# A hybrid decoder step on one core: the sample's attention moved from one 64-column block to four 32-column groups of the array

## The reference

```python
s = jnp.einsum("bqhd,bkhd->bhqk", q_blk, k, preferred_element_type=jnp.float32) * scale
s = s + fq_blk[..., :, None] - fk_t[:, :, None, :]
mask = kpos[None, :] <= pos_blk[:, None]
s = jnp.where(mask, s, -jnp.inf)
pr = jax.nn.softmax(s, axis=-1)
return jnp.einsum("bhqk,bkhd->bqhd", pr.astype(v.dtype), v)
```

## Time and profile before

| | |
|---|---|
| Runs, median (lowest to highest) | 2732.44 us (2732.13 to 2733.84) |
| Profiled execution: span | 2731.8 us |
| Profiled execution: own time | not given apart from its span; the span is 0.6 us under the median of the runs |
| TensorE products (PE) | 2691.7 us busy, 99%, 16935 records |
| Weight loads (PEld) | 2633.0 us, 96% |
| VectorE (DVE) | 1402.5 us, 51% |
| ScalarE (ACT) | 842.8 us, 31% |
| The eight pairs | from 1221 to about 1810 us, 73 to 74 us each |

### The profile page before, as it was taken

One profiled execution on the slowest core, in us unless ns is written; L12 is line 12 of the kernel. 1 busy time (PEld: TensorE's weight loads), 2 busy tenths in 40 slices (PEclk: granted clock), 3 DMA queues, 4 the chain that ended last, 5 costly groups with the idle time before them and its releaser, 6 DMA issues.

```text
span 2731.8 us, 39716 instructions
## 1 busy us (share of the span) xinstructions
PE 2691.7 (99%) x16935; PEld 2633.0 (96%) x16935; DVE 1402.5 (51%) x1960; ACT 842.8 (31%) x1291; POOL 128.8 (5%) x98
## 2 busy tenths in 40 slices
PE   8999999999999999999999999999999999999998
PEld 8999999999999999989989999899999999999998
DVE  6877355244244244347776776756443443442444
ACT  6766321021111111324554455543111211211121
POOL 1000100000000000120000010002000000000000
PEclk9999999999999999999999999999999999999999
DMA  3113111111111111233333333411111111111112
GB/s 132 47 39 107 45 47 40 56 47 40 49 46 42 54 47 35 83 118 94 91 99 98 94 102 98 134 36 55 47 42 54 47 37 52 47 44 52 47 38 81
DMA packets 94354, 174.92 MB, mean 64 GB/s; under 512 B 18402, under 2 KB 55490, under 8 KB 94050
## 3 DMA queue, kind: packets, MB, share of 16 engines
q1 hardware_dynamic: 94178, 172.38, 20.2%
HBM read 145.92 MB, written 18.02 MB: 60 GB/s over the span
## 4 chain that ended last, share of the span: by engine, by line
PE 92%; DVE 4%; ACT 1%; issue 1%; SPq 1%; DMA 0%; DVEq 0%; ACTq 0%
PE psum L421 70%; PE psum L1241 8%; PE psum L1355 2%; PE psum L1385 2%; PE psum L1315 2%; PE psum L1288 2%; PE psum L1328 1%; PE psum L1270 1%; DVE PTL L1829 1%; DVE SB L1811 1%; ACT PTH L1026 0%; DVE QHL L1762 0%; DVE X L1959 0%; ACT SB L1001 0%; PE psum L1102 0%
## 5 line engine op out<-in xcount | busy, mean ns | idle before, releaser
L399 ACT ACTIVATE WH<-WR 128x1024 fp32r<-128x1024 f32 (+2 forms) x221 | 216.2, 978 | 1022.2 <-PE psum L421 973.4
L421 PE MATMUL psum<-XH,WH 128*128 128x352 f32 x2376 | 515.2, 325 | 5.3 <-DVE WL L412 5.3
L421 PE MATMUL psum<-XH,WL 128*128 128x352 f32 x2376 | 512.5, 323 | 0.0
L421 PE MATMUL psum<-XL,WH 128*128 128x352 f32 x2376 | 512.1, 324 | 0.0
L421 PEld LDWEIGHTS psum<-XH,WH 128*128 128x128 f32 x2376 | 405.3, 189 | 5.7 <-DVE WL L412 5.4
L421 PEld LDWEIGHTS psum<-XH,WL 128*128 128x128 f32 x2376 | 408.4, 188 | 0.0
L421 PEld LDWEIGHTS psum<-XL,WH 128*128 128x128 f32 x2376 | 404.1, 188 | 0.0
L1677 DVE TENSOR_TENSOR X<-psum,X 128x1056 f32<-128x1056 f32 x63 | 79.2, 1257 | 371.1 <-PE psum L421 371.1
L412 DVE TENSOR_TENSOR WL<-WR,WH 128x1024 fp32r<-128x1024 f32 (+2 forms) x221 | 246.5, 1115 | 13.7 <-ACT WH L399 13.7
L421 PE MATMUL psum<-FYH,WH 128*128 128x352 f32 x1134 | 245.3, 324 | 0.0
L421 PE MATMUL psum<-FYH,WL 128*128 128x352 f32 x1134 | 244.4, 323 | 0.0
(11 more groups left out here) (267 smaller groups left out, 3739.3 us busy)
## 6 DMA issues: line engine op xcount, KB each, us to landing
WR<-in_wfi SPq DMA_DIRECT2D x96, 512.0 KB, 3.5
WR<-in_wfo SPq DMA_DIRECT2D x64, 384.0 KB, 3.1
WR<-in_wa SPq DMA_DIRECT2D x24, 512.0 KB, 3.5
WR<-in_wqkv SPq DMA_DIRECT2D x24, 512.0 KB, 4.2
X<-in_xT SPq DMA_DIRECT2D x16, 528.0 KB, 5.5
CC<-in_ck SPq DMA_DIRECT2D x128, 64.0 KB, 1.8
CC<-in_cv SPq DMA_DIRECT2D x128, 64.0 KB, 1.9
x_scratch<-X SPq DMA_DIRECT2D x8, 528.0 KB, 6.5
```

The lines of the kernel that those rows point to most:

```text
L399: nc.scalar.activation(WH[:, par, 0:n], WR[:, par, 0:n], ACT.Copy).then_inc(w_hi, 1)
L421: mm = nc.tensor.matmul(psum[0:m, 3 * slot + c, 0:CH], w, x[:, k, c * CH:(c + 1) * CH], start=(k == 0 and part == 0), stop=(k == nk - 1 an ...
```

## The change

The rows of unit 0 now lie over all 128 partitions: four groups of 32 rows (`DG`, `DR`), each with two neighbouring sequences (16 rows) and 16 rows that are not used. The product of sequence b goes with 32 columns of weights to the column group b // 2 of the array (`tile_position`), and in the products with the cache the sequences come in the order 0, 2, 4, 6, 1, 3, 5, 7. In `decode_product` the loop over pages is now outside that over sequences. `SEL`, `QD`, `PTN`, the two page transposes, `DM` and what VectorE and ScalarE read of unit 0 have 128 rows or columns instead of 64; `QXd` and the two `PTX` are smaller (320 numbers per partition instead of 576 and 512). `SEL`, `QD` move to another place in SBUF. The number of products stays the same.

```diff
+DG = 4
+DR = P // DG
+DEC_ORDER = [0, 2, 4, 6, 1, 3, 5, 7]
...
-        QXd = at("QXd", [P, DB, DB * 2 * DS + 2 * DS], F32, o_c)
-        QX = QXd[:, :, :].rearrange("p a b -> p (a b)")[:, 0:2 * NS * DB].rearrange("p (b c) -> p b c", b=DB)
-        DM = at("DM", [2 * NS, DK], F32, o_c + 4 * 576)
+        QXd = at("QXd", [P, DG, 2, DR + 2 * DS], F32, o_c)
+        QX = QXd[:, :, :, :].rearrange("p g i c -> p g (i c)")
+        QD = at("QD", [P, DG, DR], F32, o_c + 4 * 320)
+        SEL = at("SEL", [P, P], F32, o_c + 4 * 448)
+        DM = at("DM", [P, DK], F32, o_c + 4 * 576)
...
+        def dec_weights(x, b):
+            return x[:, b // 2, DR * (b % 2):DR * (b % 2 + 1)]
...
-                    rows, n = (2 * NS, DK) if v == 0 else (P, P * (UNIT_OF[v][1] + 1))
+                    n = DK if v == 0 else P * (UNIT_OF[v][1] + 1)
...
-                        nc.scalar.activation(dec_home(c), O_ps[0:2 * NS, 0:P], ACT.Copy).then_inc(dec_out, 1)
+                        nc.scalar.activation(dec_home(c), O_ps[:, 0:P], ACT.Copy).then_inc(dec_out, 1)
...
-                        nc.tensor.matmul(S_ps[0:2 * NS, 0:DK], SEL[:, :], DFc[:, :], start=True, stop=False,
+                        nc.tensor.matmul(S_ps[:, 0:DK], SEL[:, :], DFc[:, :], start=True, stop=False,
                                          skip_group_check=True)
-                        for b in range(DB):
+                        for b in DEC_ORDER:
                             pe.wait_ge(cc_ld[b], 32 * (2 * c + 1) + 128 * t)
-                            nc.tensor.matmul(S_ps[0:2 * NS, 0:PAST], QX[:, b, :], CC[:, b, :],
-                                             start=False, stop=False, skip_group_check=True)
-                        nc.tensor.matmul(S_ps[0:2 * NS, PAST:DK], QD[:, :, :, :].rearrange("p b h j -> p (b h j)"),
+                            nc.tensor.matmul(S_ps[DR * (b // 2):DR * (b // 2 + 1), 0:PAST], dec_weights(QX, b),
+                                             CC[:, b, :], start=False, stop=False, skip_group_check=True,
+                                             tile_position=(0, DR * (b // 2)))
+                        nc.tensor.matmul(S_ps[:, PAST:DK], QD[:, :, :].rearrange("p g r -> p (g r)"),
                                          KS[:, SEQ:T], start=False, stop=True,
...
                         for g in range(2):
-                            nc.tensor.transpose(to[:, 2 * NS * g:2 * NS * (g + 1)],
-                                                sb(c, 0)[0:2 * NS, PAGE * g:PAGE * (g + 1)],
-                                                ident[0:2 * NS, 0:2 * NS])
-                        nc.tensor.transpose(to[0:NS, 4 * NS:6 * NS], sb(c, 0)[0:2 * NS, PAST:DK],
-                                            ident[0:2 * NS, 0:2 * NS]).then_inc(t_done, 1)
+                            nc.tensor.transpose(to[:, P * g:P * (g + 1)], sb(c, 0)[:, PAGE * g:PAGE * (g + 1)],
+                                                ident[:, :])
+                        nc.tensor.transpose(to[0:NS, NPG * P:(NPG + 1) * P], sb(c, 0)[:, PAST:DK],
+                                            ident[:, :]).then_inc(t_done, 1)
...
-                    nc.tensor.matmul(O_ps[0:2 * NS, 0:P], PTN[:, :], VN[:, :],
+                    nc.tensor.matmul(O_ps[:, 0:P], PTN[:, :], VN[:, :],
                                      start=True, stop=False, skip_group_check=True)
-                    for b in range(DB):
-                        pe.wait_ge(cc_ld[b], 32 * (2 * c + 2) + 128 * t)
-                        for g in range(NPG):
-                            mm = nc.tensor.matmul(O_ps[0:2 * NS, 0:P], PTX[g][:, b, :],
+                    for g in range(NPG):
+                        for b in DEC_ORDER:
+                            if g == 0:
+                                pe.wait_ge(cc_ld[b], 32 * (2 * c + 2) + 128 * t)
+                            mm = nc.tensor.matmul(O_ps[DR * (b // 2):DR * (b // 2 + 1), 0:P], dec_weights(PTX[g], b),
                                                   CC[:, b, PAGE * g:PAGE * (g + 1)],
-                                                  start=False, stop=(b == DB - 1 and g == NPG - 1),
-                                                  skip_group_check=True)
+                                                  start=False, stop=(b % 2 == 1 and g == NPG - 1),
+                                                  skip_group_check=True, tile_position=(0, DR * (b // 2)))
...
-                    nc.tensor.transpose(O_ps[:, P:P + 2 * NS], dec_home(c),
-                                        ident[0:2 * NS, 0:2 * NS]).then_inc(dec_t, 1)
+                    nc.tensor.transpose(O_ps[:, P:2 * P], dec_home(c), ident[:, :]).then_inc(dec_t, 1)
```

More of the change, by code:

```diff
@@ L209, in hybrid_step_kernel @@
         DFc = at("DFc", [P, DK], F32, o); o += 4 * DK
-        SEL = at("SEL", [P, 2 * NS], F32, o); o += 8 * NS
-        QD = at("QD", [P, DB, 2, DS], F32, o); o += 8 * NS
         assert o <= end_y
         CC = at("CC", [P, DB, PAST], F32, o_u)
-        QXd = at("QXd", [P, DB, DB * 2 * DS + 2 * DS], F32, o_c)
-        QX = QXd[:, :, :].rearrange("p a b -> p (a b)")[:, 0:2 * NS * DB].rearrange("p (b c) -> p b c", b=DB)
-        DM = at("DM", [2 * NS, DK], F32, o_c + 4 * 576)
+        QXd = at("QXd", [P, DG, 2, DR + 2 * DS], F32, o_c)
[3 more added lines that the diff above has]
+        DM = at("DM", [P, DK], F32, o_c + 4 * 576)
         VN = at("VN", [NS, P], F32, o_p + 8 * SEQ)
-        PTN = at("PTN", [NS, 2 * NS], F32, o_p + 8 * SEQ + 4 * P)
-        PTXd = [at(f"PTX{g}", [P, DB, 2 * NS + 2 * DS], F32, o_p + 4 * SEQ + 8 * NS * DB * g) for g in range(NPG)]
-        PTX = [y[:, :, :].rearrange("p a b -> p (a b)")[:, 0:2 * NS * DB].rearrange("p (b c) -> p b c", b=DB)
-               for y in PTXd]
+        PTN = at("PTN", [NS, P], F32, o_p + 8 * SEQ + 4 * P)
+        PTXd = [at(f"PTX{g}", [P, DG, 2, DR + 2 * DS], F32, o_p + 4 * SEQ + 8 * NS * DB * g) for g in range(NPG)]
+        PTX = [y[:, :, :, :].rearrange("p g i c -> p g (i c)") for y in PTXd]
         C0 = at("C0", [P, DK], F32, o_p)
@@ L757, in pair @@
                 for g in range(NPG):
-                    nc.gpsimd.memset(PTX[g], 0.0).then_inc(ptx_zero, 1)
+                    nc.gpsimd.memset(PTXd[g][:, :, :, :], 0.0).then_inc(ptx_zero, 1)
                 for r in (4, 5, 6):
@@ L1720, in _ @@
             lo_weights(dve, J_FG + 3)
-            nc.vector.memset(QXd[:, :, :], 0.0).then_inc(qx_zero, 1)
-            nc.vector.memset(QD[:, :, :, :], 0.0).then_inc(qx_zero, 1)
+            nc.vector.memset(QXd[:, :, :, :], 0.0).then_inc(qx_zero, 1)
+            nc.vector.memset(QD[:, :, :], 0.0).then_inc(qx_zero, 1)
             dve.wait_ge(job_done, J_QKV + 2)
@@ L1994, in _constants @@
     cn = np.concatenate([np.zeros((NS, PAST)), np.where(own, -1.0 / SCALE, 0.0)], axis=1)
-    rb, rj = np.arange(2 * NS) // (2 * DS), np.arange(2 * NS) % DS
+    row = np.arange(P)
+    used = row % DR < 4 * DS
+    rb, rh, rj = 2 * (row // DR) + row % DR // (2 * DS), row % (2 * DS) // DS, row % DS
     seen = (rb[:, None] == b[None, :]) & (j[None, :] <= rj[:, None])
-    dm = np.concatenate([np.zeros((2 * NS, PAST)), np.where(seen, 0.0, NEG)], axis=1)
-    row = np.arange(P)
-    rh = np.arange(2 * NS) // DS % 2
-    sel = np.stack([(row[:, None] // NH == rb[None, :]) & (row[:, None] % NH == 2 * hp + rh[None, :])
+    dm = np.concatenate([np.zeros((P, PAST)), np.where(seen | ~used[:, None], 0.0, NEG)], axis=1)
+    sel = np.stack([(row[:, None] // NH == rb[None, :]) & (row[:, None] % NH == 2 * hp + rh[None, :]) & used[None, :]
                     for hp in range(NHP)])
```

45 lines of the change are left out of this document (25 added, 20 removed).

## The result

The changed kernel takes **2707.41 us** (median of four runs, 2705.95 to 2712.04), the kernel before, measured beside it, 2732.3 (2732.13 to 2733.84). The ratio is **0.991, with a 95% interval of 0.990 to 0.992**: 25 us less. The profiled execution's span fell from 2731.8 to 2704.6 us, by 27.2; its own time is 2706.39. The forecast was 2717.5, with a range of 2699 to 2734.

A forecast was written before the change was run, and what follows sets the result against it. TensorE was taken to bound the kernel, busy 2691.7 of 2731.8 us. Savings of 10.5 + 1.7 + 0.8 + 2.0 = 15.0 us gave 2716.8, and with 0.6 for the median 2717.5 us; range 2699 to 2734.

The forecast's parts named there:

- no overlap: Rival: logits as before, decode product slower in later pairs by 3.5 us over seven pairs; 2734 us, chance 0.16.
- all four groups at once: Rival: halves of different products overlap freely in logits and decode product, 31.5 us saved; 2701 us, chance 0.13.
- Overlap, the unknown: Step for logits and decode product: starts keep order, giving one product per record length, plus 0.025 us per weight load.
- the forecast's own case: Whole kernel: one product per record length, 15.0 us saved, 2717.5 us; chance 0.50, own range 2711 to 2727.
- Logits: Sixteen records of logits(0) take 2.14 us instead of 3.46: 1.32 less a pair, 10.5 us over eight pairs.
- Decode product, pairs 0 to 6: Values' loads decide: pair 1 saves 0.9, pair 4 loses 0.4, middle 0.25 saved; 1.7 us over seven pairs.
- Decode product, pair 7: At the lower clock, saving between 0 and 2.5 us; 0.8 taken, with the same loads in the way.
- Tile sizes: Tile-size changes: turn(0) 0.16 us less, decode_turn 0.17 less, L1284 0.08 more; net 0.25 per pair, 2.0 us.
- Exposed weight loads: Rival: in both loops each record waits for its own weight load, 0.03 to 0.095 us; 2757 us, chance 0.07.
- absorption: Rival: chains behind the transposes become due at once, more waits, half the gain stays; 2725 us, chance 0.10.
- a clock under 1.00: Sign of being wrong in pairs 0 to 6; rival: clock drops to 1.2 GHz in each pair, 2738 us, chance 0.04.
- second rival: Second in the prediction's list of rivals: no overlap, 2734 us, chance 0.16.

The follow-up runs named there:

- one group for both: Changed kernel with the cache products of both logits(0) and decode_product put to column group 0: 2736.16 us, ratio 1.0018 to the kernel before.
- natural order: Changed kernel with the sequences in the order 0 to 7 in both loops: 2704.44 us, ratio 0.9901 to the kernel before.

## Why the prediction was right and wrong

The direction, the bound and the place of the new wait were right; the size was not, 25 us instead of 15. That the time lies in the stated range says little, since the range ran from no overlap to all four groups at once. **The step that failed is in "Overlap, the unknown": "if starts keep their order, the next product can't start before the second half of this one has".** They don't keep it across groups. The second record of a product waits for the first, but it doesn't hold up the others. The rival "all four groups at once" (2701, chance 0.13) had the mechanism. The argument against that rival, two halves in one group, was right about the halves and wrong about what follows from them.

What stood in the place of evidence was the sequence of records in the earlier trace rows. Those records are all in one column tile, where start order and waiting for each other can't be told apart. So the forecast's own case should not have had four times the chance of that rival.

- *Logits.* 10.5 us forecast, 18.4 measured: 2.30 a pair instead of 1.32. The rival's 0.87 + 0.08 us for the sixteen records is 1.00, under the 1.2 us that the prediction had named as a sign of being wrong. The small weight loads cost less than was taken, 24 ns once, behind the first batch of four, and not 25 ns for each of eight products. `SEL` was taken to cost what it did before; it takes 0.09 us more a pair.
- *Decode product, pairs 0 to 6.* 1.7 forecast, 5.7 measured (28.0 to 22.3 us). That the loads decide was right, 8.4 us of new wait, in the middle of the product. What stands behind the last load was 0.77 us, not 1.45: the same failed step. Pair 1 ended 1.8 us after its first record where 2.7 was forecast and 1.9 was the rival's, pair 4 3.8 where 4.0 and 3.2 were. The product now takes between 1.8 and 3.8 us from pair to pair, a wider scatter than its mean gain of 0.8, and the forecast had read it from two pairs. (Its time without a wait, 2.5 us, adds up to 2.4; nothing hangs on it.)
- *Decode product, pair 7.* 0.8 forecast, 4.3 measured. But 2.4 of that had been lost before it, by VectorE's passes at L1906 and a clock that fell earlier. The prediction costed VectorE and ScalarE at nothing from their slack in a whole pair. In the last pair, without projection steps between, that cover is gone, and this was missed. The loads that it had taken to be in the way here were not: TensorE came to the product after the last had landed.
- *Tile sizes.* 2.0 forecast. `turn(0)` is shorter by 0.18 per pair and `decode_turn` by 0.29, from the start of the transpose before it to that of the second product behind it (0.57 to 0.28); 0.16 and 0.17 were forecast. That is 3.8 us in all. L1284 costs 0.06 more a pair, where 0.08 was forecast. Against them, with one group for both, the logits' stretch is 2.1 us longer than before and the product's 3.5, part of it waiting; in the pairs nothing is left of the 2.0.
- *The other rivals.* No overlap was given 2734; made on purpose, with one group for both, it is 2736.16. Exposed weight loads fell: with all products in one group records keep 0.216 and 0.109. The clock stayed at 1.00 outside pair 7, but for pair 2, where it fell for 3.4 us behind a wait for a load: the prediction's sign of a clock under 1.00 came once in seven pairs, not in each. Of absorption, the wait at L1842 did not grow in the changed kernel; it grew from 3.9 to 8.7 us once the loads were out of the way.

On the two rules of the Trainium skill that the prediction weighed: the trace goes with "TensorEngine Tiling (Array Packing)", section Theoretical Speedup, up to four times: the sixteen records of the logits, with the last one's 0.22 us, took 3.46 us and take 0.91. "TensorE: Matmul & The Clock Gate", part 3, says that matmuls are never reordered. Here a record that had to wait for its group was passed by records of the other groups that stand behind it in the program. The measurement decides: between groups of columns that order doesn't hold. The prediction says that the sum by "up to four times" is that of its second rival; it is that of "all four groups at once", which stands first in its list.

## What to carry to other kernels

Products of 32 columns of weights can be made four at a time by spreading their outputs over the four column groups, also where each is an fp32 product of two records; the order in the program hardly matters as long as no more than four records of one group stand in a row. When a product gets four times faster, look at once for what feeds it and what follows it: here its loads kept 11 of some 36 us. A second queue that took four of the sixteen won that back, but only where nothing that was due stood behind its issues. And a slack averaged over a stage is no cover in the one repetition of it that has no filler.

## What was new about the hardware

- Records of four column groups start 6 to 7 ns apart (13 to 14 where neighbours share a group), each streaming at its full rate, 0.216 us for 256 columns, and the groups don't slow each other: sixteen records in 1.00 us, thirty-two of 128 columns in 1.02.
- A record that waits for its group is overtaken by others of other groups. One running and three waiting records per group are passed; a fifth holds up the stream. The limit was seen in one product (pair 7, at 1.2 GHz), and from the other side in the natural order, where four in a row cost nothing.
- Nothing passed a wait for a semaphore: in pair 1 fourteen records ran, then none started for 0.63 us until sequence 7 was there, though of the eight page-1 products behind it all but that of sequence 7 had their values.
- SyncE's queue issues these loads at some 0.47 us each (7.60 us for sixteen in pair 1 of the changed kernel). On ScalarE's queue they take 0.46 us each: an exponential behind them was held up, and passes that were already on their way ran beside them.
- VectorE's normalisation of 288 columns takes 0.37 us alone and 1.4 to 1.7 us where it begins during a GpSimd pass of 1.90 us over `WR`. In the kernel before it took 0.36 us in pairs 0 and 7, which have no such pass, and 0.5 to 0.9 us in pairs 1 to 6, where it began near the end of one.
